# Entering each layer of a two-layer hybrid decoder on the un-rooted input: six projection groups scaled by the row root afterwards, the normalized rows made beside them

## What is computed

```
def _rmsnorm(x, g):
    y = x * lax.rsqrt(jnp.mean(x * x, axis=-1, keepdims=True) + NORM_EPS)
    return y * g
...
hn = _rmsnorm(h, g_mix_pre) * valid[None, :, None]
u = (hn @ w_in).astype(F32)          # then split into q, k, v, gates, ...
```

## Time and profile before

| what | value |
|---|---|
| median of three runs | 978.7 us (978.58 to 979.68) |
| the profiled execution, its own time | 978.57 us |
| its span, first to last instruction | 976.4 us |
| TensorE busy | 963.8 us (99%) |
| VectorE busy | 590.7 us (60%) |
| ScalarE busy | 512.5 us (52%) |
| GpSimd busy | 79.6 us (8%) |
| mean granted TensorE clock | 0.998 |

### The profile page before, as it was taken

How to read it: one execution, slowest core, us unless ns; L and a number is a source line. 1 busy time by engine, 2 the same in 40 slices (tenths; PEclk the granted TensorE clock), 3 DMA queues, 4 the chain that set the end, 5 groups by cost and what they waited for, 6 DMA issues and landing times.

```text
span 976.4 us, 19018 instructions
## 1 busy us (share of the span) xinstructions
PE 963.8 (99%) x7450; PEld 908.1 (93%) x7450; DVE 590.7 (60%) x894; ACT 512.5 (52%) x822; POOL 79.6 (8%) x72
## 2 busy tenths in 40 slices
PE   8999999999999999999999999999999999999998
PEld 6999888899999999999979999888999899999886
DVE  7566575367857655553456675654679566665543
ACT  6543744475466544444445546544754765544542
POOL 1000000000031222210100000000000312122000
PEclk9999999999999999999999999999999999999999
DMA  6875334346562655555544664433465635656652
GB/s 192 279 231 161 118 115 130 112 125 161 164 208 73 194 172 172 173 182 183 156 129 147 186 184 130 131 113 117 143 180 167 191 122 182 194 191 195 213 174 86
DMA packets 164299, 158.02 MB, mean 162 GB/s; under 512 B 9603, under 2 KB 157294, under 8 KB 163854
## 3 DMA queue, kind: packets, MB, share of 16 engines
q1 hardware_dynamic: 163118, 153.76, 51.0%
q10 hardware_dynamic: 928, 3.33, 1.0%
q0 software_dynamic: 192, 0.07, 0.0%
HBM read 154.98 MB, written 1.05 MB: 160 GB/s over the span
## 4 chain that ended last, share of the span: by engine, by line
PE 92%; DVE 4%; ACT 2%; DMA 1%; issue 1%; ACTq 0%; DVEq 0%; SPq 0%
PE banks L684 24%; PE banks L686 24%; PE banks L685 24%; PE banks L1059 2%; PE banks L1061 2%; PE banks L1060 2%; PE banks L734 2%; PE banks L719 1%; PE banks L715 1%; PE banks L716 1%; DVE lo L1521 1%; PE banks L926 1%; PE banks L924 1%; DVE term L1817 1%; PE banks L664 1%
## 5 line engine op out<-in xcount | busy, mean ns | idle before, releaser
L684 PE MATMUL banks<-xh,hi 128*128 128x272 f32 (+1 forms) x1584 | 457.2, 289 | 0.2
L1521 DVE TENSOR_TENSOR lo<-raw,hi 128x1024 fp32r<-128x1024 f32 (+1 forms) x288 | 349.0, 1215 | 174.1 <-ACT hi L1146 173.6
L686 PE MATMUL banks<-xh,lo 128*128 128x272 f32 (+1 forms) x1584 | 452.9, 286 | 0.0
L685 PE MATMUL banks<-xl,hi 128*128 128x272 f32 (+1 forms) x1584 | 451.9, 285 | 0.0
L1146 ACT ACTIVATE hi<-raw 128x1024 fp32r<-128x1024 f32 (+1 forms) x288 | 301.6, 1048 | 118.5 <-PE banks L686 43.2
L684 PEld LDWEIGHTS banks<-xh,hi 128*128 128x128 f32 x1584 | 298.5, 188 | 6.6 <-issue 4.7
L686 PEld LDWEIGHTS banks<-xh,lo 128*128 128x128 f32 x1584 | 298.6, 189 | 0.0
L685 PEld LDWEIGHTS banks<-xl,hi 128*128 128x128 f32 x1584 | 298.3, 188 | 0.0
L1236 ACT ACTIVATE gates<-banks,par 128x272 f32<-128x272 f32 (+1 forms) x64 | 30.7, 480 | 98.2 <-PE banks L686 91.1
L1967 POOL TENSOR_TENSOR silu_g<-silu_g,rstd 128x272 f32<-128x272 f32 (+1 forms) x44 | 54.6, 1240 | 216.7 <-ACT silu_g L1411 216.7
L1960 POOL TENSOR_TENSOR sq<-sq 128x272 f32<-128x272 f32 (+1 forms) x18 | 21.3, 1185 | 608.6 <-ACT sq L1396 608.0
(11 more groups left out here) (272 smaller groups left out, 1253.3 us busy)
## 6 DMA issues: line engine op xcount, KB each, us to landing
raw<-in_w_in SPq DMA_DIRECT2D x54, 1024.0 KB, 5.2
raw<-in_ffn_w_gate SPq DMA_DIRECT2D x22, 1024.0 KB, 5.3
raw<-in_ffn_w_up SPq DMA_DIRECT2D x22, 1024.0 KB, 5.3
raw<-in_ffn_w_down SPq DMA_DIRECT2D x19, 1024.0 KB, 5.1
raw<-in_w_out SPq DMA_DIRECT2D x8, 1024.0 KB, 5.1
raw<-in_w_in SPq DMA_DIRECT2D x12, 512.0 KB, 4.2
raw<-in_w_branch SPq DMA_DIRECT2D x12, 512.0 KB, 5.4
raw<-in_ffn_w_down SPq DMA_DIRECT2D x4, 768.0 KB, 4.4
```

The lines of the kernel that those rows point to most:

```text
L684: mm(dst, wh, mh, start=start, stop=False)
L685: mm(dst, wh, ml, start=False, stop=False)
L686: return mm(dst, wl, mh, start=False, stop=stop)
L1521: tt(half_of(lo, g, c), half_of(raw, g, c), half_of(hi, g, c).bitcast(F32), ALU.subtract).then_inc(lo_ready, 2 if g in G_MIX else 1)
```

## The change

The six groups small, mqk0, mqk1, gr, rg and gqk of each layer are made from `uh`, `ul` (the input times gain, un-rooted), and VectorE scales them by the root when it takes them out of PSUM. The normalized tiles `xh`, `xl` for the later groups are made two per group, one a half, beside mqk1, gr, rg and gqk. Layer 0's `small` is made in true fp32 from `hT` and weights times gain. `mqk1`'s second half gets PSUM bank 5 where it had bank 0. Parameters are transposed between the fourth and fifth input tile. The products of ones ahead of the first groups go. `add_sublayer` adds a tile before the low part of the tile ahead. Convolution and rotation steps move one to three groups back.

```diff
@@ order of the steps
-           ("group", "gr"), ("load_tables", 1), ("conv", 0), ("group", "rg"), ("load_tables", 2), ("conv", 1), ("group", "gqk"),
-           ("conv", 2), ("group", "rq"), ("conv", 3), ("group", "rk"), ("conv_silu",),
-           ("group", "mv"), ("rot", 0), ("rot", 1),
-           ("group", "gv"), ("turn", "mv"), ("rot", 2), ("rot", 3),
-           ("group", "rv"), ("turn", "gv"), ("group", "sbq"), ...
+           ("group", "gr"), ("load_tables", 1), ("group", "rg"), ("load_tables", 2), ("group", "gqk"),
+           ("conv", 0), ("group", "rq"), ("conv", 1), ("group", "rk"), ("conv", 2), ("group", "mv"), ("conv", 3),
+           ("group", "gv"), ("conv_silu",), ("turn", "mv"), ("rot", 0), ("rot", 1),
+           ("group", "rv"), ("turn", "gv"), ("rot", 2), ("rot", 3), ("group", "sbq"), ...
@@ banks and lags
-WARM_START, WARM_FIRST, WARM_NORM, WARM_PRE = 8, 4, 4, 3
+WARM_START, WARM_NORM = 8, 4
-FIRST_BANKS, MQK1_BANKS, ... = (0, 1, 7), (4, 0), ...
-FIRST_LAGS = ((0, 3, 6), (0, 0, 3))
+FIRST_BANKS, MQK1_BANKS, ... = (0, 1, 7), (4, 5), ...
+FIRST_LAGS = ((0, KT), (0, 0, 3))
+X_AT, PAR_AT = (0, 1, 2, 3, 6, 7, 8, 9), (4, 5)
+DEFERRED = ("mqk1", "gr", "rg", "gqk")
+NORMAL_FROM = "rq"
@@ TensorE
+            def small_first(t):
+                ps = open_tile(t)
+                for k in range(KT):
+                    if k % 4 == 0:
+                        pe.wait_ge((hi_ready, lo_ready)[k // 4], 2)
+                    wait_taken(pe, X_AT[k])
+                    last = mm(ps[:, 0:T], small_scaled[:, k, :], hT[:, k, :], start=k == 0, stop=k == KT - 1)
+                close_tile(last, t)
             def first(l):
-                together([(t, g, 0), (t + 1, g + 1, 0), (t + 2, g + 1, 1)], in_step(FIRST_LAGS[l]), xh, xl, 0, ...)
+                if l == 0:
+                    small_first(t)
+                    mean_square_first()
+                    together([(t + 1, g + 1, 0), (t + 2, g + 1, 1)], in_step(FIRST_LAGS[l]), uh, ul, 0, *ready)
+                else:
+                    together([(t, g, 0), (t + 1, g + 1, 0), (t + 2, g + 1, 1)], in_step(FIRST_LAGS[l]), uh, ul, 0, *ready,
+                             mean_square(l, 0, 0))
             def group(l, name):
+                if name == NORMAL_FROM:
+                    pe.wait_ge(xh_ready[l], 2 * KT)
+                    pe.wait_ge(xl_ready[l], 2 * KT)
+                mh, ml = (uh, ul) if name in DEFERRED else (xh, xl)
             def gate(l):
-                wait_taken(pe, group_tile(l, "small"))
+                pe.wait_ge(small_ready, l + 1)
             for l in range(DEPTH):
-                if l:
-                    mean_square(l, 0, 0)
-                    keep_warm(WARM_PRE)
-                else:
-                    mean_square_first()
-                    keep_warm(WARM_FIRST)
@@ ScalarE
+            def round_in(l, k):
+                ...
+                fn(uh[:, k, :], hT[:, k, :], ACT.Copy, scale=par[:, l, R_MIXPRE + k:R_MIXPRE + k + 1]).then_inc(xh_ready[l], 1)
+                if l:
+                    square_h(l, 0, k, 0)
             def first(l):
                 for j in range(2):
-                    ... (the three evacuations)
                     round_half(half + 2 + j)
+                wait_taken(act, group_tile(l, "small"))
+                fn(M["small"][:], M["small"][:], ACT.Identity, bias=ifbias[:, l:l + 1]).then_inc(small_ready, 1)
             def group(l, name):
                 for j in range(2):
+                    if name in DEFERRED:
+                        round_x(l, 2 * DEFERRED.index(name) + j)
+                        if name in QUERY_ONLY:
+                            wait_taken(act, t + j)
+                            fn(gate, gate, ACT.Silu)
+                        ... (the round_half calls as before)
+                        continue
                 if l == 0:
                     square_first()
-                    round_half(0)
+                    act.wait_ge(bias_loaded, 48)
+                    diagonals()
+                    for k in range(KT):
+                        round_in(l, k)
+                        if k == 3:
+                            round_half(2)
+                            round_half(3)
                     root(l, 0, 0)
-                    act.wait_ge(bias_loaded, 48)
+                    round_half(4)
+                    round_half(5)
                 else:
-                    round_half(2 * G_MIX[l] + ROUND_AHEAD - 1)
+                    half = 2 * G_MIX[l] + ROUND_AHEAD
+                    round_half(half - 1)
                     for k in range(KT):
-                        square_h(l, 0, k, 0)
+                        round_in(l, k)
+                        if k == 2:
+                            round_half(half)
+                    round_half(half + 1)
                     root(l, 0, 0)
-                round_x(l)
@@ VectorE
+            def normal(l, n):
+                stt(sq[:, n, :], hT[:, n, :], par[...], rstd[:], ALU.mult, ALU.mult).then_inc(xn_ready[l], 1)
+                for k in range(max(n - 1, 0), n + n // (KT - 1)):
+                    dve.wait_ge(xh_ready[l], KT + k + 1)
+                    tt(xl[:, k, :], sq[:, k, :], xh[:, k, :].bitcast(F32), ALU.subtract).then_inc(xl_ready[l], 1)
+            def rest_of_in(l, k):
+                dve.wait_ge(xh_ready[l], k + 1)
+                stt(ul[:, k, :], hT[:, k, :], par[...], uh[:, k, :].bitcast(F32), ALU.mult, ALU.subtract).then_inc(xl_ready[l], 1)
+                if l and k == 1:
+                    rest_of_half(2 * G_MIX[l] + REST_AHEAD)
+            def scaled(l, t, dst, q0=0, factor=None):
+                wait_tile(dve, t)
+                ... (one tensor_tensor: dst = bank * rstd)
             def add_sublayer(l, n, q0, behind=None):
-                for k in range(2, KT):
+                for k in range(1, KT):
                     scale(k)
                     if behind:
+                        add(k)
                         behind(k - 1)
-                        add(k)
             def first(l):
-                rest_of_half(2 * g + REST_AHEAD + 2)
+                dve.wait_ge(rstd_ready[l], 1)
+                scaled(l, t, M["small"][:])
+                for j in range(2):
+                    scaled(l, t + 1 + j, M["conv_in"][:, j, 3:])
+                rest_of_half(2 * g + REST_AHEAD + 3)
                 if l:
                     pads(l)
-                rest_of_half(2 * g + REST_AHEAD + 3)
             def group(l, name):
-                rest_of_half(2 * g + REST_AHEAD)
-                rest_of_half(2 * g + REST_AHEAD + 1)
+                for j in range(2):
+                    if name in DEFERRED:
+                        normal(l, 2 * DEFERRED.index(name) + j)
+                        scaled(l, t + j, into(name, j, q0), ...)
+                    rest_of_half(2 * g + REST_AHEAD + j)
+            for k in range(KT // 2):
+                turned_in(k)
+            for l in range(DEPTH):
+                params_in(l)
+            scale_small(0, hi_ready)
+            for k in range(KT // 2, KT - 1):
+                turned_in(k)
+            scale_small(1, lo_ready)
+            turned_in(KT - 1)
+            for k in range(2):
+                input_rest(k)
+            rest_of_half(2)
+            for k in range(2, KT):
+                input_rest(k)
+            rest_of_half(3)
             for l in range(DEPTH):
-                if l:
-                    rest_of_half(2 * G_MIX[l] + REST_AHEAD)
-                pre_norm(l)
+                for n in range(2):
+                    rest_of_half(2 * G_MIX[l] + ROUND_AHEAD + n)
-                    add_sublayer(l, 3, q0)
+                    add_sublayer(l, 3, q0, lambda k: rest_of_in(l + 1, k))
```

More of the change, by code:

```diff
@@ L279, in last_of @@
         put(bank)
-    free(*RING, *RING, *RING[:DEPTH])
+    free(*(RING * 3)[:KT + DEPTH])
     for l in range(DEPTH):
@@ L407, in build @@
         assert end <= conv_at + 4 * 4 * (T + 3)
+        (uh,), end = tenants(b0, [("uh", [P, KT, T], F32R)])
+        assert end <= conv_at
+        (ul,), _ = tenants(b0 + sum(room(s) for n, s in mix_spec if n != "osb"), [("ul", [P, KT, T], F32R)])
         (yh,), e1 = tenants(b0, [("yh", [P, 8, T], F32R)])
@@ L455, in build @@
         x_loaded = [sem(f"x_loaded{i}") for i in range(2)]
-        sq_ready = [[sem(f"sq_ready{n}_l{i}") for n in range(4)] for i in range(DEPTH)]
+        sq_ready = [[sem(f"sq_ready{n}_l{i}") if i or n else None for n in range(4)] for i in range(DEPTH)]
         out_rows, out_stored = sem("out_rows"), sem("out_stored")
@@ L736, in tile @@
                         close_tile(last, t)
-                if n == 2:
+                if n % 2 == 0:
                     return tile
-                if n == 0:
-                    for k in range(KT):
-                        tile(k)
-                else:
-                    pe.wait_ge(sq_summed[l], n // 2 * (KT - 2) + KT - 2)
-                    tile(0)
-                    tile(KT - 1)
```

(39 more changed lines are left out.)

120 lines of the change are left out of this document (61 added, 59 removed).

## The result

The changed kernel takes 973.44 us, median of 11 runs (971.05 to 977.87), where the kernel before takes 979.37 beside it (11 runs, 978.58 to 981.16): a ratio of 0.9939, interval 0.9926 to 0.9952. That is faster, by 5.9 us of the 7.6 forecast, and the time lies within the range of 968.3 to 974.7. The runs are spread over 7 us where those of before are spread over 2.6. The profiled execution took 972.89, with a span of 970.5.

What follows compares the result with a forecast made beforehand. TensorE, 92% of the chain, was taken to bound the kernel, with time to gain at both layers' entrances. -5.4 - 2.8 + 0.6 = -7.6 on 978.57 gave 971.0 us, range 968.3 to 974.7.

Steps and rivals of the forecast that it cites:

- case (A): The forecast itself, both entrances shorter and 0.3 us lost before each `rq`: 971.0 us, own range 970.0 to 972.3, chance 0.54.
- rival D: Layer 0's start hangs on late biases, parameters or small weights; 1 to 3 us late give 972 to 974; chance 0.10.
- Layer 0's entrance, 5.4 forecast: At the start of layer 0, mqk1's first matmul moves from 27.85 to 22.4 us, 5.4 saved.
- small start 11.4: In layer 0's entrance, `small` takes the seventh input tile's bank, free at 11.4 us, and starts then.
- the diagonals began later than 9.5: Sign against the forecast at layer 0's start: ScalarE's diagonals later than 9.5 us would make it wrong.
- Nothing stalls, so I take the full clock: In layer 0's entrance, TensorE's inputs come in time from `small` through mqk0, so its clock is not halved.
- Layer 1's entrance, 2.8 forecast: At the layers' boundary, mqk1 moves from 520.83 to 518.05, 2.8 us saved, with a stall of about 1.1.
- Hidden: In the four groups after each entrance, VectorE's added work, about 2.3 us a half against TensorE's 3.03, costs nothing.
- Halves are still 4 us early: In the four groups, weight loads issued up to 2 us later, landing in 5.2, still give halves 4 us early.
- `rq`, 0.3 a layer: Before `rq`, the last low part is done 3.0 us behind, wanted at 2.8; 0.3 lost in each layer.
- Granted clock 1.00 throughout: Sign for the forecast: TensorE's clock stays at the full rate; 0.50 in either entrance would make it wrong.
- The 7.6 of the sum: Whole kernel: 5.4 and 2.8 us saved at the two entrances, 0.6 lost before `rq` in both layers together.

Runs made afterwards that it cites:

- the run alone: New entrance and deferred groups for layer 0 only, layer 1 as before, against the kernel before: 976.08 us, ratio 0.9965.
- copies-first: Changed kernel with VectorE's copies of the fifth to eighth input tile ahead of both scalings of the small weights: 974.85 us, ratio 0.9957 to the kernel before.
- run 1: The changed kernel repeated unaltered, against the kernel before: 974.31 us, ratio 0.9938.
- the run with five ones: Changed kernel with five products of ones at the start instead of eight, nothing in their place: 973.60 us, ratio 0.9941 to the kernel before.
- the two kernels that free it: Changed kernel with gqk's last two normalized rows rounded first: 972.42 us; that plus ones spread among transposes and VectorE's low part before the evacuation: 972.35 us.
- experiment 2: Changed kernel with ScalarE taking the output projection's tile out of PSUM before rounding the next weight half: 975.14 us, ratio 0.9953 to the kernel before.

## Why the prediction was right, and where not

**The mechanism of case (A) came true, with a smaller sum.** The time lies above the 970.0 to 972.3 that (A) had as its own range, and inside the whole range only, where rival D's 972 to 974 lie. Step by step:

- **Layer 0's entrance, 5.4 forecast, 4.4 in the profile, 3.4 in the median of the run alone.** Durations were right (scaling 0.69 for 0.7, `small` 3.93 for 3.7, sums and halves to 0.1). The step that failed is "small start 11.4": it began between 11.6 and 12.8 in eleven profiles. Two things hold it in turn. Where the products of ones end late, the transposes begin at 7.5 to 8.1 and the first scaling at 10.4 to 11.0, without a wait; where they end early (5.5 to 6.9), the scaling waits for the small weights, for which no landing time was worked out, until 9.7 to 10.75 (the profile of copies-first apart). Rival D named the small weights; it was the right doubt at too low a chance. Its other doubt, the biases, held nothing: the diagonals began later than 9.5, which the prediction had named as a sign against itself, in three profiles (9.54 to 9.65), and in two of those mqk1 still began at 23.49.
- **"Nothing stalls, so I take the full clock"** held in the profile of after but not in run 1 (half the rate over 6.99 us) and in part not in the run with five ones. Behind the transposes and 1.00 and 1.44 us of idle the clock was at 0.50 in these two profiles, and at 1.00 in three others behind 1.18 to 1.44 us. The Trainium skill (TensorE: Matmul & The Clock Gate, Part 4: PE-mode transpose) has it that a transpose doesn't count as busy in the way of a matmul. By that rule `small` would be at risk in every run; two of the eleven profiles with the new start show it. The mean clock that each run reports goes with its time: the seven runs of the changed kernel at 0.999 or 1.000 took 971.05 to 974.00, the ten below that 972.89 to 977.87. It doesn't tell where in a run the clock fell.
- **Layer 1's entrance, 2.8 forecast:** 2.6 to mqk1, 2.7 to the gate, 24.39 to 24.42 from the boundary's sums to the gate in all eleven profiles that have it, where before has 27.07. mqk1 began there at 513.41, for 512.95 in the prediction. The stall was placed right and sized 1.1 for 0.9.
- **"Hidden", for the four groups:** right for VectorE's work (0.68 idle in most halves), wrong for the loads. "Halves are still 4 us early" did not hold: in the profile of after ScalarE waits 1.47 us for a load in gqk that took the usual 5.3. The late issue had spent the margin, and a load of 8.69 then reached TensorE.
- **`rq`, 0.3 a layer:** right in size where the load is in time (no wait above 0.3 in the profile of after); 0.8 and 3.3 in layer 0 of two later profiles. The sum had the common case of an edge whose tail is long. That this edge makes a large part of the spread is shown by the two kernels that free it: their ten runs lie between 971.27 and 973.17, where ten of the changed kernel's seventeen lie above 973.2.
- **Not in the prediction: the 2.2 us at layer 1's output,** with the fall of the clock behind it. The stretch from the gate to the head sums of layer 1 gained 0.7 where 0.3 was to be lost, and the chain there is loads of 5.4 and 6.75 us with roundings between. The wait follows the landing of the one load of FFN weights: 0.3 to 0.6 where it took 5.2 to 5.5 us (five profiles, both of before among them), 1.2 where it took 6.15, 1.9 to 2.2 where it took 6.5 to 6.75 (seven; the order of experiment 2 left out). Why it lands late is open, and so is whether the change brings it about: two profiles of before without it stand against eight of eleven with it (1.2 or more). "Granted clock 1.00 throughout" fails at this place in the profile of after.

The 7.6 of the sum and the 5.9 measured differ by 1.0 at the start and 2.2 at the output, less 1.5 gained in between, in stretches to which the sum gave losses of 0.3 or nothing; where those 1.5 come from was not tested. The two profiles of before differ by 0.3 and 0.2 in the two longest of these stretches, so a part can be chance. Without the 1.5 the time would be some 974.9 (an estimate from these differences), just above the range: luck has a part in its holding.

## What to carry to other kernels

Where work is deferred beside a stream of loads, look at what the new edge stands behind in each engine's own order: a rounding of 0.4 us behind a wait for a landing inherits the landing's whole tail. Put what the next stage waits for ahead of what waits for memory; here that took a spread of 7 us in seventeen runs to 2 us in ten (one of 1 us in the five with this edit alone). And price a load by its longest landing in that stretch, not by its median, whenever the change issues it later.

## What was not expected of the hardware

- A 1 MB weight load takes 5.2 us as a rule, but 8.69 from issue to landing in one profile. A table load of the same size ran beside it, as one did in the changed kernel, where the same load took 5.3.
- The granted clock falls at different places in runs of one kernel: at 11.8 to 18.6 us in one profile, only at 770.7 to 774.2 in another, nowhere before the last microseconds in the profiles of four variants (mean clock 1.000). The kernel before has it at 17.8 to 21.2 and at 20.3 to 23.7. Behind the wait of 1.9 to 2.2 us at layer 1's output it fell in four profiles and stayed at 1.00 in three.
- 13 us of work added to VectorE over sixteen halves cost about 5 us of time in the median; TensorE never waited in these halves, and 3.6 us at the two edges behind them.
